# Where a weight unit's split into high and low parts stands in the order of the attention stages, and in how many steps the compressed softmax is cut

## The reference, cut to what matters

```python
def first_block(x, w_in, ...):                  # 2 layers
    h = x @ w_in[l]                             # 9216 columns
    o_a = retention(rq, rk, rv, rg)
    o_b = chunk_attention(cq, ck, cv)
    o_c = diff_attention(dq, dk, dv)
    merged = sum(sigmoid(gates_n + b_merge_n) * (o_n @ w_branch_n))
    x = layer_norm(ALPHA * x + merged @ w_out[l]); x = layer_norm(ALPHA * x + swiglu(x))
def second_block(x, ...):                       # 2 layers
    x = layer_norm(ALPHA * x + 0.5 * swiglu(x))
    proj = x @ w_in[l]                          # conv, gmlp, q, k, v, gates
    pc = masked_softmax(q @ kc, cmp_end <= t)   # "compressed" branch: 15 keys
    o_cmp = pc @ vc                             # beside it: 2 more branches, o_s and o_w
    mix = concat(y_conv, y_gmlp, y_nsa) @ w_out[l]
    x = layer_norm(ALPHA * x + mix); x = layer_norm(ALPHA * x + 0.5 * swiglu(x))
```

## Time and profile before

| | us |
|---|---|
| median of 3 timed runs (2116.33 to 2117.65) | 2116.69 |
| the profiled execution | 2115.45 |
| its span | 2113.6 |
| PE busy | 2053.4 (97%), 14392 matmuls |
| DVE busy | 1239.1 (59%), 1534 instructions |
| ACT busy | 926.5 (44%), 1278 instructions |
| chain that ended last | PE 92%, DVE 4%, ACT 2%, DMA 1% |
| granted TensorE clock, mean | 0.992 |

### The profile page before, as it was taken

How to read it: one execution, slowest core, us unless ns; L and a number is a source line. 1 busy time by engine, 2 the same in 40 slices (tenths; PEclk the granted TensorE clock), 3 DMA queues, 4 the chain that set the end, 5 groups by cost and what they waited for, 6 DMA issues and landing times.

```text
span 2113.6 us, 32608 instructions
## 1 busy us (share of the span) xinstructions
PE 2053.4 (97%) x14392; PEld 1880.2 (89%) x14392; DVE 1239.1 (59%) x1534; ACT 926.5 (44%) x1278; POOL 47.6 (2%) x76
## 2 busy tenths in 40 slices
PE   7999999999999999999999999899999999989998
PEld 6889998999798999899899988789999998878997
DVE  5555655555655565655655565565565556656555
ACT  3444544444444443444444454344444445434442
POOL 0000000000000000000000001000000000100000
PEclk9999999999999999999999999999999999999999
DMA  7534455765444455576566653258656665425663
GB/s 268 180 122 154 152 183 146 210 196 182 166 156 138 146 174 170 166 221 188 166 179 182 197 140 124 72 154 231 188 166 180 181 196 137 147 86 154 180 193 106
DMA packets 415894, 352.60 MB, mean 167 GB/s; under 512 B 28704, under 2 KB 360840, under 8 KB 415624
## 3 DMA queue, kind: packets, MB, share of 16 engines
q1 hardware_dynamic: 415752, 350.51, 55.0%
HBM read 349.43 MB, written 1.05 MB: 166 GB/s over the span
## 4 chain that ended last, share of the span: by engine, by line
PE 92%; DVE 4%; ACT 2%; DMA 1%; issue 0%; POOL 0%; DVEq 0%; SPq 0%
PE ps L201 28%; PE ps L202 28%; PE ps L203 27%; PE ps L1360 2%; PE ps L1498 2%; PE ps L1440 1%; PE ps L1475 1%; DVE hl L1878 1%; DMA raw<-in_w_in 1%; DVE tm L1944 1%; PE ps L1478 1%; ACT hl L1639 1%; DVE xt L1953 0%; ACT tm L1681 0%; PE ps L1536 0%; PE ps L1480 0%
## 5 line engine op out<-in xcount | busy, mean ns | idle before, releaser
L1878 DVE TENSOR_TENSOR hl<-raw,hl 128x2048 fp32r<-128x2048 f32 (+2 forms) x333 | 738.3, 2221 | 490.5 <-ACT hl L1639 490.3
L201 PE MATMUL ps<-xt,hl 128*128 128x256 f32 (+1 forms) x2672 | 756.3, 283 | 0.0
L202 PE MATMUL ps<-xt,hl 128*128 128x256 f32 (+1 forms) x2672 | 747.0, 280 | 0.0
L203 PE MATMUL ps<-xt,hl 128*128 128x256 f32 (+1 forms) x2672 | 746.7, 279 | 0.0
L1639 ACT ACTIVATE hl<-raw 128x2048 fp32r<-128x2048 f32 x324 | 615.0, 1900 | 232.0 <-PE ps L203 217.2
L201 PEld LDWEIGHTS ps<-xt,hl 128*128 128x128 f32 (+1 forms) x2672 | 502.2, 188 | 4.8 <-issue 1.7
L202 PEld LDWEIGHTS ps<-xt,hl 128*128 128x128 f32 (+1 forms) x2672 | 502.1, 188 | 4.4 <-issue 1.2
L203 PEld LDWEIGHTS ps<-xt,hl 128*128 128x128 f32 (+1 forms) x2672 | 501.9, 188 | 0.2
L201 PE MATMUL ps<-hl,o 128*128 128x512 f32 x656 | 262.3, 400 | 9.7 <-DVE o L1986 6.8
L203 PE MATMUL ps<-hl,o 128*128 128x512 f32 x656 | 259.4, 395 | 0.0
L202 PE MATMUL ps<-hl,o 128*128 128x512 f32 x656 | 259.4, 395 | 0.0
(11 more groups left out here) (197 smaller groups left out, 1677.5 us busy)
## 6 DMA issues: line engine op xcount, KB each, us to landing
raw<-in_w_in SPq DMA_DIRECT2D x84, 1024.0 KB, 5.1
raw<-in_w_ffn_in SPq DMA_DIRECT2D x88, 512.0 KB, 5.2
raw<-in_ffn_gate SPq DMA_DIRECT2D x88, 512.0 KB, 4.0
raw<-in_ffn_up SPq DMA_DIRECT2D x88, 512.0 KB, 5.3
raw<-in_ffn_down SPq DMA_DIRECT2D x44, 1024.0 KB, 5.1
raw<-in_w_ffn_out SPq DMA_DIRECT2D x22, 1024.0 KB, 5.1
raw<-in_w_out SPq DMA_DIRECT2D x16, 1024.0 KB, 5.1
raw<-in_w_branch_a SPq DMA_DIRECT2D x8, 1024.0 KB, 5.2
```

Source lines behind the costliest of these rows:

```text
L201: e.matmul(out, l[0], r[0], start=start, stop=False)
L202: e.matmul(out, l[0], r[1], start=False, stop=False)
L203: return e.matmul(out, l[1], r[0], start=False, stop=stop)
L1878: e.tensor_tensor(lo[:, c], m["raw"][:, k % NRAW, 0:n][:, c], hi[:, c].bitcast(F), ALU.subtract).then_inc(s.low.up(("low", k), *([("low", ...
```

## The change

`unit` gets a flag `spread`. With it no `need` stands before the unit; instead, behind the unit's second piece stands `need_high` (load and whole high of the units that are due, as a rule g+2), behind its third piece the first half of their low, and behind its fourth the second half. Three places use it: `n_parts`, `t_parts` and `lin_v`. Besides the attention parts (110 units) this takes in the up units of the feed-forward, which call `t_parts` through `t_unit` (120 units): 230 of 324 units have the new form, and by the list of steps they start 239 units, two at once at nine places (the first such unit behind each of nine layer norms). The gates' unit, the feed-forward's down units, `out_end` and the units of the layer norms keep the old form. In `compressed(i)` two steps of cost 0.0 are added, after `cmp_exp` and after `cmp_mask`, and `compressed(1)` is let go by `turned` (the `weigh` step of the last task) where it was let go by `full11`.

```diff
-    def unit(self, segs, n):
+    def unit(self, segs, n, spread=False):
         g = len(self.units)
         self.units.append((segs, n))
-        self.add("need", g + self.ahead)
+        if not spread:
+            self.add("need", g + self.ahead)
         return g
+
+    def spread(self, g, piece):
+
+        if piece == 1:
+            self.add("need_high", g + self.ahead)
+        elif piece in (2, 3):
+            self.add("need_low", piece - 2)
@@ settled
+            if kind == "need_low":
+                for u in due:
+                    out.append(("low", (u, self.units[u][1], args[0], 2)))
+                if args[0]:
+                    due.clear()
+                continue
+            if kind == "need_high":
+                assert not due
+                while k < min(len(self.units), args[0]):
+                    due.append(begin())
+                continue
@@ n_parts (t_parts and lin_v likewise)
-        g = P.unit(segs, n)
+        g = P.unit(segs, n, True)
         for i in range(2):
             for k0 in (0, 2):
                 add("n_part", ...)
+                P.spread(g, 2 * i + k0 // 2)
@@ compressed
                 add("cmp_exp", l, i, er, mx)
                 yield 0.5
+                yield 0.0
                 add("cmp_mask", l, i, er, rs)
                 yield 0.2
+                yield 0.0
                 tb, et = PB.take(), ET.take()
@@ nsa
-                         at.until("full02"), lambda: finish(0), at.until("full11"), lambda: compressed(1))
+                         at.until("full02"), lambda: finish(0), at.until("turned"), lambda: compressed(1))
```

More of the change, by code:

```diff
@@ L338, in settled @@
     def settled(self):
-        out, k, low = [], 0, {}
+        out, k, low, due = [], 0, {}, []
         def begin():
@@ L348, in settled @@
         for kind, args in self.steps:
+            if kind == "need_low":
[9 more added lines that the diff above has]
+                continue
+            assert not due or kind not in ("need", "prep")
             if kind == "need":
@@ L461, in t_parts @@
                 add("t_part", g, n, nk, view, banks[-1], c, k0, last, src, src_events, after)
+                P.spread(g, (c * nk + k0) // 4)
                 if not last:
@@ L1029, in lin_v @@
                      w_in[:, 2176 + g * 256:2176 + g * 256 + 128].rearrange("(k p) c -> p k c", p=128)) for g in range(2)]
-            g = P.unit(segs, UNIT)
+            g = P.unit(segs, UNIT, True)
             bk = PB.take()
@@ L1034, in lin_v @@
                     add("kv_values", g, bk, i, k0, xt_events(P.xv))
+                    P.spread(g, 2 * i + k0 // 4)
                     if i == 0 or k0 == 0:
```

## The result

The changed kernel takes 2120.0 us (median of 20 runs, 2118.2 to 2121.5) against 2116.7 us of the kernel before on the same chip: ratio 1.0018, 95% interval [1.0012, 1.0024]. It is a little slower; I had forecast 2107.7. The profiled execution has a span of 2118.2 us, 4.6 more than before.

The account below looks back on a forecast made before the run. PE, busy 97% of the span, bounds the kernel, so only its stops and slow clock can be won. Terms -3.2 - 4.6 - 4.8 + 2.1 + 1.0 + 0.5 = -9.0 give 2106.4, as median 2107.7 us; range 2103.5 to 2113.5.

Parts of the forecast that it names:

- Stops 1 and 2: NSA, both layers: PE's waits for the bank L1890 frees and for the compressed softmax's mask go, 3.2 and 4.6 us.
- Stop 3 grows: NSA, PE's wait for turned probabilities behind the convolution: 4.6 us instead of 3.51, as score matmuls move behind it; +2.1 us.
- The clock: NSA: layer 0 runs like layer 1 without its slow matmuls, giving back 4.8 us; ends 0 and 4.8.
- Start: Start of the kernel: load 2 moves behind twelve setup DMAs; +0.5 us, ends -0.4 and +1.8.
- The new stop at layer 1's first block: Unit 83 starts two units at once, so the first one's second half comes late; +1.0 us, ends 0.7 and 1.3.
- First block's attention: First block's attention: the split only comes later, with about 1 us to spare at the tightest place; cost 0.
- feed-forward: The six feed-forward starts: four halves end about 0.6 us ahead of need; cost 0, without that cover 0.2 each.
- start of NSA: First NSA units: halves are ready just before PE needs them, cover 0.3 us; cost 0, without it some 0.5 a layer.
- halves as such: 239 more units cut in halves add some 24 us of DVE work, for which PE doesn't wait; cost 0.
- D: Rival, no change: the stop at the turned probabilities takes what the first two stops give; 2118 us, chance 0.09.
- B: Rival: the stops go but the clock doesn't come back, or another 1 to 2 us wait replaces them; 2112.5, chance 0.20.
- C: Rival, slower: late second halves make PE wait in the first block's attention, 16 places a layer; 2132 us, chance 0.06.

Follow-up runs that it names:

- e2: Spread of the splitting alone on the kernel before: no extra steps in the compressed softmax, compressed(1) released at full11; 2107.07 us, ratio 0.9966.
- e3: Kernel before with only the compressed softmax's part changed (two extra steps, release at turned), units split the old way; 2125.72 us, ratio 1.0049.
- e1: Changed kernel with one word put back: compressed(1) is released at full11 again, not at turned; 2109.88 us, ratio 0.9971.
- e6: Changed kernel with the convolution's DVE and ACT steps moved behind the last transposes of the two score groups; 2091.60 us, ratio 0.9895.
- e7: Spread alone (e2), but the very first weight unit releases the old way, its load ahead of the set-up's DMAs; 2106.18 us, ratio 0.9957.
- e9: e6 with two weight units, the first of all and the first of layer 1's first block, releasing the old way; 2090.47 us, ratio 0.9875.
- e12: Kernel before with only the softmax part (two extra steps, release at turned) and the convolution's steps moved last, old splitting; 2109.51 us, ratio 0.9968.
- e11: e6 with the feed-forwards' up units (120 of the 230 spread ones) releasing the old way; 2092.62 us, ratio 0.9886.

## Why the prediction was wrong, step by step

**Stops 1 and 2: right.** Both went, in both layers (7.8 us). The reason given for stop 2 had a part too many: either half of the change does it alone, the spread in e2 and the softmax part in e3, which both have no wait for the mask.

**Stop 3 grows: right in length, wrong in price.** It grew by 1.00 us (3.51 to 4.51), forecast 1.07, by the mechanism named. Waits in N0 and N1 fell by 5.8 us in all; the forecast's -7.8 + 2.1 is -5.7. But I priced the growth at its own length, and set its lower end at 0 in case the clock falls earlier and comes back earlier. It did neither. In layer 0 of the kernel before it fell at 1347.4, 1.2 us before the stop ended, and was back at 1354.2; in the changed kernel it fell at 1342.9, 0.8 us behind the stop's end, and was back at 1363.4.

**The clock: the step that failed.** "With both stops gone I expect layer 0 to run like layer 1, which gives back 4.8 us." With the spread alone it does: e2's layers are equal (82.08 and 81.95) and its span is 2104.6, which is 9.0 under before. That this is the forecast's sum is luck: without the growth of stop 3, which e2 doesn't have, my terms give -11.1. But in the changed kernel both layers became like the bad one: busy 83.03 in both, against 81.61 and 76.78. That is +7.7 us where I had -4.8: 12.5 of the 13.6 us by which the span's change (+4.6) differs from the forecast's (-9.0). I had read the earlier trace rows as the price of stops 1 and 2 alone. Before, 17.1 us of layer 0 lay at 0.50 and only 6.8 of layer 1, and stop 3 was behind 6.8 in each. I knew from the earlier trace rows that the values behind it took twice their time (3.68 us), and then moved 16 short matmuls behind it for 1.07 us, without asking what the clock would do with them.

**Start: in range.** +0.5 forecast, +1.1 by the first `turn_copy` on PE (35.29 before, 36.43 after). ACT waited for the raw weights until 25.52 (before 16.94); the issue moved behind the set-up's loads, to 9.14 from 3.30, where I had put 12.4. ACT's timeline of the changed kernel:

```profile
25.52 1.92 ACT L1664 ACTIVATE hl<-raw 128x2048 fp32r<-128x2048 f32 x1 [11.26 <-DMA raw<-in_w_in]
```

**The new stop at layer 1's first block: right.** Forecast +1.0 (0.7 to 1.3); PE waits 0.76 us at 553.94, and PE's lag behind the kernel before grows by 0.86 us between there and the next stop. The three halves on DVE, against the earlier trace rows, and PE's row behind them:

```profile
550.40 3.49 DVE L1903 TENSOR_TENSOR hl<-raw,hl 128x1024 fp32r<-128x1024 f32 x3
```

```profile
553.94 0.50 PE L201 MATMUL ps<-hl,xt 128*128 128x512 f32 x1 [0.76 <-DVE hl L1903]
```

**First block's attention, feed-forward, start of NSA, halves as such: right**, at 0. L1903 runs 572 times, and its busy time costs nobody.

**Not foreseen:** the clock fell once more, behind the 1.42 us stop at 312.6, which was as long before and had no such effect (1.3 us). Added up against the span: -5.8 + 7.7 + 1.1 + 0.9 + 1.3 = +5.2, measured +4.6.

**The range:** the terms named for its low end (stop 3's growth hidden, no new stop, no cost at the start) give 2104.1 and not 2103.5. Either way it had no term for more slow time behind stop 3, which the upper end needed.

**The rivals.** D gave the measured time within 2 us (2118), but by another way: stop 3 not by its length but by the clock behind it. B had the clock as not coming back; it got worse instead. C, the slow one, did not happen. None had a stop that grows a little and, in layers that had 6.8 us of slow time behind it, makes that 20.5. That the release brings this on is what e1 and e3 show, and that it does so by way of stop 3 is what e6 shows. Why the clock comes back sooner or later behind the same stop, as in e1's two layers, is not shown.

## What to carry to other kernels

A stop of TensorE ahead of short matmuls costs its length and the half speed behind it, and here the second part was twice the first (83.03 less 73.44 us busy a layer, for a stop of 4.5); price both, for a stop that grows as for one that goes. Work moved from inside a stop to behind it is paid in full, and at half speed if the clock is down there: the scores 1.89 us for 1.07. When a change clears small waits and leaves the largest, look first at what is queued ahead of that one's releaser: moving one step that nobody needed yet (the convolution's) was worth 8 us on the kernel before, 14 on the spread and 26 or more on the changed kernel.

## What the runs showed of the hardware that I had not expected

- Half speed can outlast its cause by far: 21.40 us of 21.40 busy at a mean clock of 0.52, behind a stop of 4.51 us, and in e3 it was 23.8 us in one piece, the end of the stop and the 21.48 us busy behind it. By the Trainium skill (TensorE: Matmul & The Clock Gate, "What's actually happening") a throttled array is released soon after sustained work begins. Behind the stop at 312.6 us, among matmuls of 512 columns, the trace agrees: in the changed kernel the clock was down from 312.1 to 315.5 only. Among the short ones of N0 and N1 it doesn't, and the measurement decides: there PE was busy all the time by the profile and the clock stayed down for 20 us.
- The time of one program varies with the clock. e7 has two groups of runs some 5 us apart (mean clocks of 0.993 to 0.996 and of 0.992), and the kernel before spreads over 8 us; beside e9 to e12 its runs up to 2113.9 have 0.994 or 0.995, those from 2115.4 on 0.990 to 0.993. The kernels without stops over 0.7 us in N0 and N1 have a clock of 1.00 there in their traces, and those with the same order of work have the same length within 0.1 us (74.86 to 74.96 in e6, e9 and e11).
- The 1.42 us stop at about 312 us is followed by half clock in some kernels and not in others, with the same work around it. Windows from 312 to 315 of the changed kernel, whose stop ends at 312.60, and of e6, whose stop ends at 312.01:

```profile
312.00:315.00 3.00, 2.40 (x6) 0.51 0.03 8
```

```profile
312.00:315.00 3.00, 2.99 (x13) 1.00 0.01 2
```

The best version tried is e9: 2090.5 us, ratio 0.9875 [0.986, 0.989] to the kernel before.
